# A hybrid decoder step on one core: output projection of the prompt inside the sampled tokens' stage, pages through rings

## The chip, the cores and the metric

The kernel runs on one core of a Trainium2 chip. The metric is the device time of one execution in microseconds; three runs of the kernel before gave a median of 1904.42 us (1900.69 to 1908.21). The engines are TensorE (PE, its weight loads PEld), VectorE (DVE), ScalarE (ACT), GpSimd (POOL) and SyncE (SP, which only issues transfers here). Each works through its own program in order and waits on semaphores.

## What is computed

One inference step of a two-layer decoder trunk, for 1024 prompt tokens and for 8 x 8 sampled tokens: a short gated convolution layer, then a forgetting-attention layer over a shared K and V. The sampled tokens attend to 1024 past rows in a paged pool, eight pages of 128 rows for each of eight batches, and to themselves. Width 1024, 16 heads of 64, all in float32.

```python
def forgetting_attn_layer(x, g, w_in, w_out, attend):
    h = rmsnorm(x, g)
    q, z = jnp.split(h @ w_in, 2, axis=-1)
    o = attend(q.reshape(Bg, T, N_HEADS, HEAD_DIM))
    y = o.reshape(Bg, T, D_ATT) * jax.nn.silu(z)
    return x + y @ w_out
...
x = x + jax.nn.sigmoid(x @ w_ple_gate[i]) * (p[i].astype(x.dtype) @ w_ple_proj[i])
...
k_past = cache_k[page_table].reshape(db, -1, N_HEADS, HEAD_DIM)
v_past = cache_v[page_table].reshape(db, -1, N_HEADS, HEAD_DIM)
s_past = jnp.einsum('bqhd,bkhd->bhqk', q, k_past).astype(jnp.float32) * scale
s_past = s_past + cn_q + jnp.swapaxes(rest, 1, 2)[:, :, None, :]
p = jax.nn.softmax(jnp.concatenate([s_past, s_new], axis=-1), axis=-1)
o = jnp.einsum('bhqk,bkhd->bqhd', p[..., :P].astype(v_past.dtype), v_past)
```

## The kernel before

Activations lie transposed, features on partitions and the 1088 token columns (1024 of the prompt, 64 sampled) along the free side, in eight rows of 128 features. A product in full precision is three matmuls of a faster kind: high part of the weights with the high and the low part of the activations, then low part of the weights with the high part (`w_hi`, `w_lo`, `Hhi`, `Hlo`). ScalarE makes high parts by a copy, VectorE low parts by a subtraction. A tile is 128 output features: 8 rows x 3 blocks of columns (364, 364, 360) x 3 matmuls.

The program is written by hand engine by engine, with semaphores between them. The stages around the change, in order:

- Prompt attention, eight pairs of heads (`half_pair`, twice a pair), with dense tiles of the next pair between its steps; the last pair's second half has none left. POOL normalises the blocks of P (line 537). The gated output `yT` of a pair is stored to memory (`parked_y`, line 417); the residual stream X was parked in memory earlier.
- The sampled tokens' stage, lines 881 to 1000 on TensorE. For each batch of eight: eight pages of K are turned on TensorE (`k_turn`, line 887), copied to `KT` by ScalarE (1261) and VectorE (1647), and multiplied with the queries two pages at a time (`s_scores`, 908). A bias matmul (`s_bias`, 896) starts the scores from `Bkeys` and `Arows`. VectorE finds the maximum (1682), ScalarE does exp (1272), P is turned back (924, 921) and multiplied with the pages of V (`s_values`, 939); the output is turned (945) and gated into `zsS`.
- K pages go through four buffers, loaded by SP from line 391 or 451 once a buffer is turned. V pages have two whole sets of eight, loaded by POOL (line 542): 13 of them already during the last half pair of the prompt attention, between its normalisations, then eight after each batch. `Bkeys` and the new V rows have two buffers too. Sixteen tiny loads at line 444 bring the new keys' sums to one partition row.
- After the last batch the parked rows of `yT` and X come back, Y is split into parts (1055, 1367), and eight output projection tiles over all 1088 columns follow (`out_tiles`, lines 620 to 622), then `feed`: the turning and splitting of the layer's input embedding, a split of X, and eight gate and projection tiles. The final norm and the output transposes end the program.

## Time and profile before

| | |
|---|---|
| median of three runs | 1904.42 us |
| the profiled execution, its own time | 1904.6 us |
| its span | 1902.6 us |
| TensorE busy, share of the span | 1721.6 us, 90% |
| VectorE, ScalarE, POOL busy | 867.0, 674.3, 321.1 us |
| mean granted clock of TensorE | 0.949 |
| moved by DMA | 161.87 MB, 85 GB/s on average |

The page divides the span into 40 slices; the sampled tokens' stage is slices 31 to 35, where DMA rises to nine tenths and the granted clock of TensorE falls to six. Durations of pipelined matmuls overlap in the records, so the pace of a series is read from the differences between starts, and a busy TensorE isn't necessarily at its peak. What an engine waited for stands in brackets behind a row, with the idle time before it.

### The profile page before, as it was taken

How to read it: one execution, taken by the hardware profiler on the slowest of the kernel's cores; microseconds unless marked ns; L12 is line 12 of the kernel's file. 1: busy time of each engine (PE TensorE's matmuls, PEld its weight loads, DVE VectorE, ACT ScalarE, POOL GpSimd, SP SyncE). 2: the span in 40 equal slices, each digit the busy share in tenths (PEclk: the TensorE clock that was granted, in tenths of full speed). 3: DMA queues.
4: the chain of work that ended last, by engine and by line, in shares of the span. 5: the costliest groups of instructions: out<-in, count | busy, mean ns of one | idle time of the engine just before them, and what ended most of it. 6: DMA issues, size and time to landing. Idle time of an engine off the chain costs nothing.

```text
span 1902.6 us, 31400 instructions
## 1 busy us (share of the span) xinstructions
PE 1721.6 (90%) x11034; PEld 1584.1 (83%) x11034; DVE 867.0 (46%) x1361; ACT 674.3 (35%) x1094; POOL 321.1 (17%) x335
## 2 busy tenths in 40 slices
PE   6999999999999859999999999999865888899997
PEld 5999999999989759888888888888643555598997
DVE  4433333343253484555565555555543333423443
ACT  5111111111053233555655556565531232302322
POOL 4111111100000021322222122222121222000110
PEclk8999999999999879999999999999866999899998
DMA  4111111111201203211101021110235799821102
GB/s 142 46 46 45 46 44 45 44 36 44 76 28 44 88 19 93 58 46 35 57 23 59 21 79 45 34 57 24 68 144 173 281 373 362 303 68 41 42 28 94
DMA packets 165110, 161.87 MB, mean 85 GB/s; under 512 B 19661, under 2 KB 141661, under 8 KB 164935
## 3 DMA queue, kind: packets, MB, share of 16 engines
q1 hardware_dynamic: 154566, 126.38, 21.0%
q0 software_dynamic: 10496, 34.88, 5.0%
q8 instruction: 28, 0.46, 0.1%
q14 instruction: 20, 0.16, 0.0%
HBM read 137.41 MB, written 23.81 MB: 85 GB/s over the span
## 4 chain that ended last, share of the span: by engine, by line
PE 74%; DVE 9%; issue 5%; ACT 5%; DVEq 2%; DMA 2%; ACTq 1%; SPq 1%; POOL 1%; POOLq 0%
PE PS L620 14%; PE PS L622 14%; PE PS L621 14%; PE PS L781 4%; PE PS L782 4%; PE PS L783 4%; PE PS L840 3%; PE PS L887 3%; PE PS L828 2%; PE PS L939 2%; PE PS L811 2%; DVE small L1522 2%; DVE pTl L1533 2%; PE PS L812 1%; PE PS L908 1%
## 5 line engine op out<-in xcount | busy, mean ns | idle before, releaser
L620 PE MATMUL PS<-Hhi,w_hi 128*128 128x364 f32 (+1 forms) x1536 | 513.1, 334 | 36.2 <-DVE Hlo L1367 32.9
L622 PE MATMUL PS<-Hhi,w_lo 128*128 128x364 f32 (+1 forms) x1536 | 510.7, 333 | 0.0
L621 PE MATMUL PS<-Hlo,w_hi 128*128 128x364 f32 (+1 forms) x1536 | 510.3, 332 | 0.0
L620 PEld LDWEIGHTS PS<-Hhi,w_hi 128*128 128x128 f32 x1536 | 294.9, 192 | 41.1 <-issue 29.1
L621 PEld LDWEIGHTS PS<-Hlo,w_hi 128*128 128x128 f32 x1536 | 295.0, 192 | 0.0
L622 PEld LDWEIGHTS PS<-Hhi,w_lo 128*128 128x128 f32 x1536 | 294.2, 192 | 0.0
L781 PE MATMUL PS<-Hhi,w_hi 128*128 128x364 f32 (+1 forms) x768 | 274.6, 358 | 0.1
L782 PE MATMUL PS<-Hlo,w_hi 128*128 128x364 f32 (+1 forms) x768 | 252.6, 329 | 0.0
L783 PE MATMUL PS<-Hhi,w_lo 128*128 128x364 f32 (+1 forms) x768 | 252.6, 329 | 0.0
L505 POOL TENSOR_TENSOR w_raw<-w_raw,GT 128x1024 f32<-128x1024 f32 x65 | 127.1, 1956 | 697.2 <-DMA w_raw<-in_w_kv 385.6
L1014 ACT ACTIVATE w_hi<-w_raw 128x1024 fp32r<-128x1024 f32 (+1 forms) x97 | 105.5, 1089 | 371.2 <-PE PS L622 368.5
L1317 DVE TENSOR_TENSOR w_lo<-w_raw,w_hi 128x1024 fp32r<-128x1024 f32 (+1 forms) x97 | 125.9, 1298 | 78.7 <-ACT w_hi L1014 76.4
L1533 DVE TENSOR_TENSOR pTl<-PS,pTh 128x512 fp32r<-128x512 f32 x192 | 103.6, 555 | 126.0 <-ACT pTh L1159 123.7
L537 POOL TENSOR_SCALAR Pb<-Pb,small 128x128 f32<-128x128 f32 (+7 forms) x128 | 97.3, 764 | 365.1 <-DVE small L1527 365.0
L1151 ACT ACTIVATE Pb<-PS,small 128x128 f32<-128x128 f32 (+7 forms) x128 | 94.8, 741 | 161.3 <-DVE small L1522 161.3
L781 PEld LDWEIGHTS PS<-Hhi,w_hi 128*128 128x128 f32 x768 | 147.1, 192 | 0.9 <-DVE w_lo L1317 0.4
L782 PEld LDWEIGHTS PS<-Hlo,w_hi 128*128 128x128 f32 x768 | 146.2, 190 | 0.0
L783 PEld LDWEIGHTS PS<-Hhi,w_lo 128*128 128x128 f32 x768 | 145.1, 189 | 0.0
L1159 ACT ACTIVATE pTh<-PS 128x512 fp32r<-128x512 f32 x192 | 89.9, 488 | 99.9 <-PE PS L828 96.6
L1522 DVE TENSOR_REDUCE small<-PS 128x1 f32<-128x128 f32 (+7 forms) x128 | 95.8, 749 | 39.3 <-PE PS L814 38.7
L887 PE MATMUL PS<-ident,Kpages 128*128 128x128 f32 x512 | 82.2, 309 | 34.0 <-ACT KT L1261 22.8
L887 PEld LDWEIGHTS PS<-ident,Kpages 128*128 128x128 f32 x512 | 62.4, 156 | 58.3 <-ACT KT L1261 25.9
(247 smaller groups left out, 2207.3 us busy)
## 6 DMA issues: line engine op xcount, KB each, us to landing
Kpages<-in_cache_k SPq DMA_DIRECT2D x64, 512.0 KB, 7.0
Vpages<-in_cache_v POOLq DMA_DIRECT2D x64, 512.0 KB, 9.8
w_raw<-in_w_in_a SPq DMA_DIRECT2D x64, 256.0 KB, 3.0
w_raw<-in_w_ple_gate SPq DMA_DIRECT2D x16, 512.0 KB, 3.7
w_raw<-in_w_kv SPq DMA_DIRECT2D x32, 256.0 KB, 3.2
w_raw<-in_w_in_b SPq DMA_DIRECT2D x32, 256.0 KB, 3.4
parked_x<-X SPq DMA_DIRECT2D x8, 544.0 KB, 5.2
X<-parked_x SPq DMA_DIRECT2D x8, 544.0 KB, 7.5
```

The source lines that it names most:

```text
L505: g.tensor_tensor(w, w, GT[:, :, r:r + 1].to_broadcast([P, KC, P]), ALU.mult).then_inc(sems["w_gained"], 1)
L620: mm(out, wh, hi[:, k, s:e], start=(k == 0), stop=False)
L621: mm(out, wh, lo[:, k, s:e], start=False, stop=False)
L622: last = mm(out, wl, hi[:, k, s:e], start=False, stop=(k == nk - 1))
L781: mm(out, wh, Hhi[:, k, s:e], start=(k == 0), stop=False)
L782: mm(out, wh, Hlo[:, k, s:e], start=False, stop=False)
L783: last = mm(out, wl, Hhi[:, k, s:e], start=False, stop=(k == KC - 1))
L887: last = tp(PS[:, c, (i % 4) * P:(i % 4 + 1) * P], Kr[:, pg % RING, i * P:(i + 1) * P], ident[:, :])
L1014: af(whi[:, par, 0:nk, :], raw[:, par, 0:nk, :], ACT.Copy).then_inc(sems["w_hi"], 1)
L1317: tt_(wlo[:, par, 0:nk, :], raw[:, par, 0:nk, :], f(whi[:, par, 0:nk, :]), ALU.subtract).then_inc(sems["w_split"], 1)
L1522: ve.reduce_max(small[:, qb:qb + 1], score_bank(qb)[:, 0:n], AXX, negate=True).then_inc(sems["rowmax"], 1)
L1533: tt_(pTl[:, kb % 2, q0 * P:512], PS[:, 5 + kb % 2, q0 * P:512], f(pTh[:, kb % 2, q0 * P:512]), ALU.subtract).then_inc(sems["p_lo"], 1)
```

## The change

The projection of the prompt's 1024 columns no longer has a stage of its own. Tile m runs during batch m+1 of the sampled tokens, in 16 pieces (2 blocks of 512 columns x 8 rows) of three matmuls that `out_pieces` puts between page turns, scores and values. Values of a batch are multiplied during the next batch's turns, a page or two per slot. So V needs a ring of four pages, as K has: POOL loads page n+4 when page n has been multiplied. `KT` holds single pages, scores are made page by page, page turns go to PSUM banks 5 and 6. `Bkeys`, `Arows` and the new V rows have one buffer each; the new keys' sums are stored so that one transfer per batch brings them. Everything moved into memory that the prompt attention uses, so K and V loads wait until its scores and its value products are done, and no V load stands in POOL's attention loop. The parked rows of `yT` come straight into `Hlo` and are split in place during batch 0; X comes back a row per batch. The sampled columns are projected at the end, from weights loaded unsplit into the buffers that have become free, in plain fp32 matmuls of 64 columns. The diff, cut to its core:

```diff
 RING = 4
 NK = KEYS + DS
...
-                        load_keys(0, pg, first=True)
+                    sp.wait_ge(sems["y_out"], START["y_out"] + 16 * (NPAIR - 1))
+                    for k in range(NPAIR - 1):
+                        sp.dma_start(f(Hlo[:, k, 0:SEQ]), d["y"][k]).then_inc(sems["y_back"], 16)
+                    return
                 sp.wait_ge(sems["o_done"], START["o_done"] + 4 * j + 4)
                 sp.sem_inc(sems["sp_step"], 1)
                 sp.dma_start(d["y"][bass.ds(j, 1)].rearrange("a p n -> (a p) n"), yT[:, 0:SEQ]).then_inc(sems["y_out"], 16)
...
-            sp.wait_ge(sems["y_out"], START["y_out"] + 16 * NPAIR)
-            sp.wait_ge(sems["kv_out"], START["kv_out"] + 64 * NPAIR)
...
-            with nc.allow_non_contiguous_dma(reason="eight values of each head, once"):
-                for x in range(2):
-                    for b in range(DB):
...
+            def load_x(m, par):
+                sp.dma_start(at_pair(X, m).rearrange("p a n -> p (a n)"), d["x"][bass.ds(m, 1)].rearrange("a p n -> (a p) n")).then_inc(sems[f"x_back{par}"], 16)
+            def sample_loads(b, par, x=True, tile=True, more=True):
+                if x:
+                    load_x(b, par)
+                for pg in range(RING, PAGES):
+                    load_keys(b, pg)
+                if tile:
+                    load(N_B2 + b + 1, (N_B2 + 1 + par) % 2, w_out_b[:, :, bass.ds(P * b + P, P)])
+                if more:
+                    for pg in range(RING):
+                        load_keys(b + 1, pg)
...
+            sp.wait_ge(sems["score"], START["score"] + 16 * NPAIR)
+            for pg in range(RING):
+                load_keys(0, pg, first=True)
+            sp.wait_ge(sems["pv"], START["pv"] + 24 * NPAIR)
+            load_x(0, 0)
+            sample_loads(0, 0, x=False, tile=False)
+            sample_loads(1, 1)
+            with sp.Fori(0, 2) as i:
+                sample_loads(2 * i + 2, 0)
...
+            sp.wait_ge(sems["s_score"], START["s_score"] + PAGES * DB)
+            load_last(0, KT[:, 0, :, :])
+            load_last(1, KT[:, 1, :, :])
...
+                sp.wait_ge(sems["s_pv"], START["s_pv"] + PAGES * DB - RING + u + 1)
+                load_last(3 + u, Vb[:, u, :].rearrange("p (k n) -> p k n", k=KC))
+            load_last(7, PsT[:, 0:PAGES, :])
...
-            def load_values(b, par, pg):
+            def load_values(b, pg):
...
-            def early_values(n):
-                for pg in range(n, n + 2):
-                    if pg < PAGES + 5:
...
-                    if not more and hh == 1:
-                        g.wait_ge(sems["s_table"], 16)
-                        g.wait_ge(sems["block_done"], START["block_done"] + B_B2)
                     for qb in range(4):
                         normalise(8 * hh + qb, j)
-                        if not more and hh == 1:
-                            early_values(2 * qb)
...
+            def later_values(b):
+                for pg in range(RING, PAGES):
+                    used(b, pg - RING + 1)
+                    load_values(b, pg)
+            def sample_loads(b, more=True):
+                if more:
+                    g.wait_ge(sems["s_all"], b + 1)
+                    g.sem_inc(sems["pool_step"], 1)
+                    load_sample(b + 1)
+                later_values(b - 1)
+                for pg in range(RING):
+                    used(b - 1, RING + pg + 1)
+                    load_values(b, pg)
+                    if pg == 1:
+                        load_new(b)
...
+            load_sample(0)
+            g.wait_ge(sems["pv"], START["pv"] + 24 * NPAIR)
+            for pg in range(RING):
+                load_values(0, pg)
...
+                        last = tp(PS[:, 5 + c, (i % 4) * P:(i % 4 + 1) * P], Kr[:, pg % RING, i * P:(i + 1) * P], ident[:, :])
...
+            def s_scores(b, par, pg):
...
+                        last = mm(SS[32 * g_:32 * g_ + 32, P * pg:P * pg + P], qc[:, par, g_, e, :], KT[:, pg % 2, 2 * g_ + e, :],
...
-            def s_values(b, par):
-                pe.wait_ge(sems["s_osb"], START["s_osb"] + b)
-                for pg in (0, 1, 2, 3, 4, PAGES, 5, 6, 7):
...
+            def s_values(b, pg):
...
-            def sample_batch(b, par, first=False, more=True):
-                k_turn(b, 4)
...
-                s_p_turn(b, 2)
-                s_values(b, par)
...
+            def out_pieces(m, par, q0, n):
...
+                    mm(PS[:, blk, :], wh, Hhi[:, k, s:s + 512], start=(k == 0), stop=False)
+                    mm(PS[:, blk, :], wh, Hlo[:, k, s:s + 512], start=False, stop=False)
+                    last = mm(PS[:, blk, :], wl, Hhi[:, k, s:s + 512], start=False, stop=(k == KC - 1))
+                    if k == KC - 1:
+                        last.then_inc(sems["block_done"], 1)
+                return q0 + n
...
+            def sample_batch(b, par, first=False):
+                q = 0
+                back = {3: (0, 1), 4: (2, 3), 5: (4, PAGES), 6: (5, 6), 7: (7,)}
+                for u in range(PAGES):
+                    if u >= 3 and not first:
+                        s_values(b - 1, back[u][0])
+                    if u == 2:
+                        if not first:
+                            for r in range(3):
+                                s_p_turn(b - 1, r, PAGES * b + 2)
+                        s_bias(b, par)
+                        s_scores(b, par, 0)
+                        if not first:
+                            q = out_pieces(b - 1, 1 - par, q, 1)
+                    k_turn(b, u)
+                    if not first:
+                        q = out_pieces(b - 1, 1 - par, q, 1 if u >= 2 else LAG_D[u])
+                    if u == 0 and not first:
+                        s_scores(b - 1, 1 - par, PAGES - 1)
+                        if not (isinstance(b, int) and b == 1):
+                            s_y_turn(b - 2)
+                    if u >= 2:
+                        s_scores(b, par, u - 1)
+                    if 3 <= u < 7 and not first:
+                        q = out_pieces(b - 1, 1 - par, q, 1)
+                        s_values(b - 1, back[u][1])
+            pe.wait_ge(sems["s_ones"], 1)
             sample_batch(0, 0, first=True)
+            pe.wait_ge(sems["h_ready"], 40)
+            sample_batch(1, 1)
...
-            out_tiles(N_B2, ED_B2, 32)
...
+            pe.wait_ge(sems["s_out"], START["s_out"] + DB)
+            pe.wait_ge(sems["w_last"], 16 * KC)
...
+            for t, w in enumerate(slots):
+                for k in range(KC):
+                    last = mm(PS[:, 2, NS * t:NS * t + NS], w[:, k, :], zsS[:, k, :], start=(k == 0), stop=(k == KC - 1))
+            last.then_inc(sems["s_b2s"], 1)
             feed(1, N_B3, EA_B3, ED_B3, 40)
...
-            def sample_batch(b, more=True):
-                for pg in range(4, PAGES):
-                    keep_keys(b, pg)
...
+            def sample_batch(b, par, i):
+                keep_keys(b, 0)
+                keep_keys(b, 1)
+                probabilities(b - 1)
+                keep_keys(b, 2)
+                keep_keys(b, 3)
+                w_hi((N_B2 + par) % 2, B_B2 + 2 * b - 2, loaded(N_B2 + par, 2, i))
+                for pg in range(4, PAGES):
+                    keep_keys(b, pg)
+            act.wait_ge(sems["o_done"], START["o_done"] + 4 * NPAIR)
+            y_hi(NPAIR - 1, yT[:, 0:SEQ])
+            w_hi(N_B2 % 2, B_B2 - 3, loaded(N_B2))
+            for pg in range(PAGES):
                 keep_keys(0, pg)
...
+                if pg == 0:
+                    act.wait_ge(sems["y_back"], 16 * (NPAIR - 1))
+                if pg < NPAIR - 1:
+                    y_hi(pg, f(Hlo[:, pg, 0:SEQ]))
...
+            for k in range(KC):
+                y_hi(k, X[:, k, 0:SEQ])
...
+            def sample_batch(b, par, i, more=True):
...
+                keep_keys(b, 0)
+                largest(b - 1)
+                if not (isinstance(b, int) and b == 1):
+                    outputs(b - 2)
+                keep_keys(b, 1)
+                probabilities(b - 1)
+                keep_keys(b, 2)
+                keep_keys(b, 3)
+                out_block(b - 1, 1 - par, mi, 0)
+                keep_keys(b, 4)
+                w_lo((N_B2 + par) % 2, N_B2 + b)
+                keep_keys(b, 5)
+                keep_keys(b, 6)
+                if more:
+                    prepare(b + 1, 1 - par)
+                keep_keys(b, 7)
+                attended(b - 1)
+                out_block(b - 1, 1 - par, mi, 1)
+            ve.wait_ge(sems["kv_out"], START["kv_out"] + 64 * NPAIR)
+            ve.memset(f(Bk[R_CN:R_MASK, :]), 0.0)
+            ve.memset(f(Bk[R_MASK:R_END, :]), 0.0)
...
+            ve.memset(f(Bk[R_CN:R_CN + 2, :]), 1.0)
+            ve.tensor_copy(Bk[R_MASK:R_END, KEYS:], maskb[R_MASK:R_END, R_MASK:R_END])
             ve.drain().then_inc(sems["s_ones"], 1)
...
+            prepare(0, 0)
+            y_lo(NPAIR - 1, yT[:, 0:SEQ], 33)
+            w_lo(N_B2 % 2, N_B2)
+            for pg in range(PAGES):
                 keep_keys(0, pg)
...
+                if pg < NPAIR - 1:
+                    y_lo(pg, f(Hlo[:, pg, 0:SEQ]), 34 + pg)
...
+            for k in range(KC):
+                y_lo(k, X[:, k, 0:SEQ], 41 + k)
+            ve.wait_ge(sems["s_b2s"], 1)
+            tt_(X[:, :, SEQ:], PS[:, 2, :].rearrange("p (m n) -> p m n", m=KC), X[:, :, SEQ:], ALU.add)
+            ve.drain().then_inc(sems["xs_done"], 1)
...
```

On TensorE, in a steady batch of the sampled tokens' stage, two page turns and the output's turn stood in a row before (`Kpages` is the ring of K pages, `Osb` the batch's output):

```order
L885 REGISTER_ALU [waits k_in0]
L887 MATMUL PS<-ident,Kpages 128x128 [waits s_kt0]
L887 MATMUL PS<-ident,Kpages 128x128 x3
L887 MATMUL PS<-ident,Kpages 128x128 [waits s_kt1]
L887 MATMUL PS<-ident,Kpages 128x128 x3
L885 REGISTER_ALU [waits k_in1]
L887 MATMUL PS<-ident,Kpages 128x128 [waits s_kt0]
L887 MATMUL PS<-ident,Kpages 128x128 x3
L887 MATMUL PS<-ident,Kpages 128x128 [waits s_kt1]
L887 MATMUL PS<-ident,Kpages 128x128 x3
L945 MATMUL PS<-ident,Osb 128x128 [waits s_pt1,s_osb]
L908 MATMUL PS<-KT,qc 32x256 [waits s_kt1,s_kt0]
```

After the change, the same engine in the fifth slot (page 4) of a batch:

```order
L943 MATMUL PS<-ident,Kpages 128x128 [waits s_kt0]
L943 MATMUL PS<-ident,Kpages 128x128 x3
L943 MATMUL PS<-ident,Kpages 128x128 [waits s_kt1]
L943 MATMUL PS<-ident,Kpages 128x128 x3
L1010 MATMUL PS<-Hhi,w_hi 128x512
L1011 MATMUL PS<-Hlo,w_hi 128x512
L1012 MATMUL PS<-Hhi,w_lo 128x512
L964 MATMUL PS<-KT,w_raw 32x128 [waits s_kt1,s_kt0]
L964 MATMUL PS<-KT,w_raw 32x128 x7
L1007 REGISTER_ALU
L1010 MATMUL PS<-Hhi,w_hi 128x512 [waits dve_evac]
L1011 MATMUL PS<-Hlo,w_hi 128x512
```

Now a piece of the projection (L1010 to L1012, `Hhi` and `Hlo` hold the prompt's gated output) stands behind each page turn and behind the scores, and a value product of the batch before ends the slot.

On POOL, at the start of the prompt attention's last half pair, the normalisations of `Pb` had V page loads between them:

```order
L542 ISA
L542 DMA Vpages<-in_cache_v 128x1024
L541 TENSOR_LOAD pt
L541 ISA x2
L542 ISA
L542 DMA Vpages<-in_cache_v 128x1024
L537 TENSOR_SCALAR Pb<-Pb,small 128x384 [waits rinv]
L541 TENSOR_LOAD pt
L541 ISA x2
L542 ISA
L542 DMA Vpages<-in_cache_v 128x1024
```

Now, from the last four normalisations of that half pair on:

```order
L573 TENSOR_SCALAR Pb<-Pb,small 128x640 [waits rinv]
L573 TENSOR_SCALAR Pb<-Pb,small 128x768 [waits rinv]
L573 TENSOR_SCALAR Pb<-Pb,small 128x896 [waits rinv]
L573 TENSOR_SCALAR Pb<-Pb,small 128x1024 [waits rinv]
L605 DMA Bkeys<-key_bias 16x1024 [waits s_ones,kv_out,s_restout,s_table]
L606 DMA Bkeys<-key_bias 16x8
```

The normalisations follow one another, and the first transfer behind them is that of the key bias. In the steady batch a V load was one of eight behind a single wait on the batch before; each has its own wait now:

```order
L585 ISA
L585 DMA few_rows<-out_v_sample 8x1024
L541 ISA
L541 TENSOR_LOAD pt
L541 ISA x2
L542 ISA
L542 DMA Vpages<-in_cache_v 128x1024
L541 ISA
L541 TENSOR_LOAD pt
```

and in the loop over batches now:

```order
L577 ISA [waits s_pv]
L577 TENSOR_LOAD pt
L577 ISA x2
L578 ISA
L578 DMA Vpages<-in_cache_v 128x1024
L615 REGISTER_ALU
L577 ISA [waits s_pv]
L577 TENSOR_LOAD pt
L577 ISA x2
```

What moved there is the release: from the end of a batch's value products to each single page's.

## Rows read from the trace of the kernel before

**Rows 1.** Stretches: length, busy (instructions) PE, PEld, DVE, ACT, POOL, clock, DMA share, GB/s.

```profile
1427.00:1454.00 27.00, 8.06 (x33) 6.24 (x34) 9.11 (x20) 2.39 (x4) 6.55 (x13) 0.56 0.52 169
1481.00:1645.00 164.00, 137.47 (x1538) 89.29 (x1536) 63.25 (x134) 46.52 (x81) 40.54 (x78) 0.92 0.93 346
1662.00:1749.00 87.00, 86.88 (x524) 86.20 (x524) 20.79 (x31) 7.63 (x7) 0.00 (x0) 1.00 0.20 61
```

**Rows 2.** Timeline, last half pair: start, us, what, count, idle before and releaser.

```profile
1396.82 1.76 PE L828 MATMUL PS<-ident,Pb 128*128 128x128 f32 x7 [3.90 <-POOL Pb L537]
```

**Rows 3.** Timeline, from the end of prompt attention to the first bias matmul.

```profile
1425.98 0.69 DVE L1542 TENSOR_TENSOR yT<-yT,zf 64x512 f32<-64x512 f32 x1
...
1428.04 1.78 DVE L1702 MEMSET Bkeys<- 72x2064 f32 x1 [0.38 <-issue]
...
1434.35 0.53 POOL L583 DMA_DIRECT2D Bkeys<-key_bias  x1 [21.75 <-DVEq L1713]
...
1440.18 11.65 SPq L444 DMA_DIRECT2D few_rows<-new_key_sums  x16
...
1453.80 1.23 PE L896 MATMUL PS<-Bkeys,Arows 72*128 72x512 f32 x3 [14.25 <-DVEq L1657]
```

**Rows 4.** Timeline of TensorE in a steady batch.

```profile
1522.66 1.04 PE L924 MATMUL PS<-ident,Ps 128*128 128x128 f32 x8
...
1525.44 2.37 PE L939 MATMUL PS<-Vpages,PsT 128*32 128x256 f32 x40
...
1529.73 1.09 PE L887 MATMUL PS<-ident,Kpages 128*128 128x128 f32 x8
...
1537.40 1.09 PE L887 MATMUL PS<-ident,Kpages 128*128 128x128 f32 x8
1538.42 1.07 PE L908 MATMUL PS<-KT,qc 128*32 128x256 f32 x16
1539.43 1.09 PE L887 MATMUL PS<-ident,Kpages 128*128 128x128 f32 x8
1542.91 3.32 PE L887 MATMUL PS<-ident,Kpages 128*128 128x128 f32 x13 [2.39 <-ACT KT L1261]
```

**Rows 5.** Timeline of a 512-column pair in the prompt attention, full clock.

```profile
1335.44 0.19 PEld L840 LDWEIGHTS PS<-pTh,VS 128*128 128x128 f32 x1
1335.60 0.39 PE L840 MATMUL PS<-pTh,VS 128*128 128x512 f32 x1
...
1335.83 0.39 PE L840 MATMUL PS<-pTl,VS 128*128 128x512 f32 x1
```

**Rows 6.** V pages' tile: issues (ns min/median/max), landing; then one issue.

```profile
L542 POOL DMA_DIRECT2D Vpages<-in_cache_v x64: 527/530/749, 1389.4 to 1613.8; - x64
...
DMA to landing us min/median/max: 3.7/9.8/15.0
...
1490.46 0.53 POOL L542 DMA_DIRECT2D Vpages<-in_cache_v  x1 [0.71 <-issue]
```

**Rows 7.** Single lines and tiles: ns min/median/max, first and last start, forms.

```profile
L1647 DVE COPY KT<-PS x64: 680/692/693, 1433.9 to 1632.4; 128x512 f32<-128x512 f32 x64
...
L1367 DVE TENSOR_TENSOR Hlo<-X,Hhi x16: 1282/1285/1293, 529.6 to 1761.9; 128x1088 fp32r<-128x1088 f32 x16
...
L756 PE MATMUL PS<-ones,LFP x56: 275/275/275, 700.1 to 707.6; 128*128 128x128 f32 x56
...
L756 PE MATMUL PS<-tri,LFP x16: 270/275/275, 699.9 to 707.8; 128*128 128x128 f32 x16
```

**Rows 8.** Timeline of TensorE, first gate tile of the last layer.

```profile
1755.05 0.67 PE L620 MATMUL PS<-Hhi,w_hi 128*128 128x364 f32 x1 [3.10 <-DVE Hlo L1367]
1755.51 0.51 PE L621 MATMUL PS<-Hlo,w_hi 128*128 128x364 f32 x1
1755.81 0.51 PE L622 MATMUL PS<-Hhi,w_lo 128*128 128x364 f32 x1
...
1769.87 0.33 PE L620 MATMUL PS<-PTh,w_hi 128*128 128x364 f32 x1
```

401 lines of the change are left out of this document (196 added, 205 removed).

## The prediction

> **What bounds the kernel now.** I read the profiled execution from its end backwards into stages, first by the table of stretches: busy time of each engine, granted clock, DMA share and GB/s. In [rows 1] the reader is to see that TensorE is the engine of every stretch, but in two manners. In the output projection (87 us from 1662) it is busy 86.88 of 87 us at clock 1.00 with DMA at a fifth: a pure TensorE stage. In the sampled tokens' stage (164 us from 1481) DMA is busy 0.93 of the time and moves 346 GB/s, and TensorE, though it shows as busy, has holes and clock 0.92. So one stage waits for data while the next only computes. The first 27 us of the sampled stage are the worst: TensorE busy 8.06 us at clock 0.56.
>
> Next the order of time around that start. [rows 2]: in the last half pair of the prompt attention, TensorE stood still for 3.90 us until POOL had normalised the fourth block; POOL was late because page loads of V stood between its normalisations. [rows 3]: attention ends at 1426.7 (1425.98 + 0.69). Then VectorE fills Bkeys with 1.78 us memsets, POOL may only then load the key bias, and SP issues 16 tiny transfers in 11.65 us; the first bias matmul starts at 1453.80 after 14.25 us of TensorE idle.
>
> Last, one steady batch on TensorE [rows 4], read by the differences of starts: turning a K page 1.02 us (1537.40 to 1538.42), scores of a pair of pages 1.01, turning P with the next bias and one pair of scores 2.78 (1522.66 to 1525.44), nine value products 4.29, and one hole of 2.39 us until ScalarE has done exp and then a KT copy.
>
> **The change, stage by stage.** The sum compares the stretch from the end of attention (1426.7) to the end of the first gate tile of the last layer, 1769.9 by the start of the next matmul, at 1769.87 [rows 8]: 343.2 us. Before and after that stretch the same instructions stand in the same order, but for a few small VectorE operations and a finer store near 716, that I count as nothing (TensorE has dense tiles there; if not hidden, 2 us).
>
> (a) *End of attention.* V page loads leave POOL's queue, so the 3.90 us hole goes. What is late next is TensorE itself, still in the scores of the fifth block until 1392.9 (1396.82 less the hole): minus 3.8. Bounds 0 and 5.
>
> (b) *Start and batch 0.* One buffer instead of two halves the memset of 1.78 [rows 3]; three of 0.9 in a row and drains give 3.2 us until the bias may load. Five POOL issues of 0.5 and a landing of at most 3.7 (the fastest V page, [rows 6]) make 9.7; bias and first scores, 11. The 16 tiny loads are gone. Now VectorE also makes the low parts of the prompt's output: per page a KT copy of 0.69 and 1.285 x 1024/1088 = 1.21 [rows 7], so 2.0 a page, 12 for the other six. At half clock TensorE itself would need 3 a page, 18. Taken 14: batch 0 takes 25 us (bounds 23 and 30). ScalarE's half is lighter; the seven parked rows were fetched long before.
>
> (c) *Batches 1 to 7.* Each now carries one projection tile: 16 pieces of three matmuls of 512 columns. One takes 0.23 us (1335.60 to 1335.83, [rows 5]), a piece 0.69, a tile 11.0. The batch's old work, by [rows 4]: 8 x 1.02 = 8.2; eight single-page scores of 0.5 = 4.0 (half the columns, twice the calls; a call could keep more than half its cost, at most +4); turns and bias 2.78 - 1.01 = 1.8; values 4.3; output turn 0.2. Together 18.5 to the rounding, with the tile 29.5. The old holes vanish for this reason: every KT copy (0.69) now has a piece and scores in front of the next need. Exp: the last scores end at 1539.43, the turn after the hole starts at 1542.91, 3.5 us later, of which some 0.6 are the KT copy; so P is ready 2.9 us after the scores, and a page turn with three pieces (3.1) now covers that. DMA per batch: 8.4 MB of pages, 1.1 of X row and weights, 0.1 of bias, 9.6 MB; at 346/0.93 = 372 GB/s that is 25.8 us, under TensorE's 29.5. I add 1.4 us for semaphores, exp and a marginal page: 30.9 us, times seven 216.3. Bounds 29.5 and 33 (the old hole of 2.39 stays and a little more). SP's queue has X rows, K pages and weights in line; none of their waits is for work that TensorE has not long done, since K is four pages (over 12 us) ahead. VectorE has some 13 us of work, ScalarE 10.
>
> The ring is the tight place. Page 4 of V may be issued when page 0 was multiplied; by the order that is two slots (each turn, two pieces, scores, two values = 3.84 us) less one product, 7.2 us ahead of its use. Of these POOL takes 0.53 + 0.71 = 1.24 [rows 6] and something for the signal; 6.0 are left for the landing. The fastest landing is 3.7, the median 9.8, the longest 15.0 [rows 6], but those are bursts of eight pages at a DMA share of 0.93; here three or four half-megabyte transfers meet, 3.7 + 2.5 = 6.2. So I take the fast end and a marginal wait (0.4 of the 1.4).
>
> By the Trainium skill, DMA: Bandwidth & Descriptors, Anatomy of one DMA, a load from POOL takes 2.0 us and its bytes over 436 GB/s, 3.2 us for a page. The trace's fastest is 3.7; by the page's figure the marginal wait goes and the sum is 3 us less.
>
> VectorE's low-part operation of a weight tile (1.2 us, from SBUF) now falls beside V loads. The 64 V issues of the kernel before took 527 to 749 ns [rows 6], so none was held up by a whole operation. [...]
>
> (d) *Tail.* Batch 7's tile has no page turns beside it: 11.0 + scores 0.5 + turns 1.2 + values 4.3 = 17.0. Exp is covered less (0.9), and pages 4 to 7 of V have only 2.8 us from release to use while weights and inputs of the last layer load too: 4.5 us. Sum 22.4, bounds 18 and 28.
>
> (e) *Junction.* The sampled columns get their own 64 fp32 matmuls, two passes each. The nearest row: 72 passes (56 and 16) with 128x128 weights and 128 columns, their starts from 699.9 to 707.8 [rows 7], 0.11 each, so 14.1 us; with half the columns at the least 7.1. Taken 10.6, and 1 for the last weights. Beside it ScalarE and VectorE split the prompt's X: 8 x 1.21 + 0.8 = 10.5, hidden. Then the add (0.7) and the turning of the layer's embedding (some 4, from the 6.4 us between the end of the old tiles, 1748.6, and 1755.05, less the two first splits): 16.3 in all, bounds 12.5 and 20.
>
> (f) *First gate tile.* Before, 14.8 us (1755.05 to 1769.87), since its first matmuls ran at the low clock, 0.30 apart (1755.51 to 1755.81), against 86.88/524 = 0.166 at the high one [rows 1]: 72 x 0.166 = 11.9. Its splits are done already, but the engine comes from a thin stretch again: 13.0. The same rise costs once more at batch 1: 1.5.
>
> Sum: -3.8 + 25 + 216.3 + 1.5 + 22.4 + 16.3 + 13.0 = 290.7 against 343.2: 52.5 us less. From the profiled execution, 1904.6 us with a span of 1902.6 (2.0 around it), that gives 1852.1. The median of the runs, 1904.42, is the same within 0.2. Put otherwise: some 95 us of tiles, as 88, go into the stage, whose batch grows from 164/7 = 23.4 to 31 us, and the start gets shorter.
>
> **Rivals.** *The ring of V waits at the median landing.* With 9.8, page 4 is 3.8 us late in each of seven batches, 26.6 us less the 3 counted: 1876 to 1879 with the tail. For it: the median row, and three transfers at once. Against it: the bursts are gone.
>
> *Slower.* Same place, bad price: if the landing is L, the wait is L - 6.0 a batch, and about L - 3.8 in the tail beyond what I count. Seven batches and the tail eat 52.5 at L = 13; slower by 0.5% needs L of 14. At the longest row, 15.0, it is 63 + 11 - 3: 1923. Against it: with DMA at 9.6 MB in 31 us or more, 310 GB/s, queues are shorter than at 346, and they shorten as the stage stretches.
>
> *The pieces don't pack.* Each piece stands behind a foreign matmul; if its first weight load (0.19, [rows 5]) is bare 16 times a batch, that is +3.0, and +21 in seven: 1873. For it: the pieces' own cadence is known only among their like. Against: turns and scores alternate in [rows 4] at no visible price.
>
> *The tile finds little room,* since TensorE was 0.84 busy there: the spans of pipelined matmuls overlap, and the true work is 18.5 of 23.4 us. If all the busy time were real (137.47 of 164 us, [rows 1]), a batch would be 19.6 + 11.0 + 1.4 = 32.0, not 30.9, and the total 1860; inside my range.
>
> **How the numbers follow.** Forecast, 1838 to 1864: 0.60. Less than 1838 (packing better, half-price scores, short junction): 0.07. Pieces don't pack: 0.13. Ring at about its median: 0.12. Ring between, no change: 0.04. Ring slower: 0.04. Low bound: batches at 29.5 (-10), start -2, tail -4, junction -4, clock -1: 1831. High bound: the old exp hole in seven batches (+14) or the ring at its median, with a long tail: 1882. A measurement can tell some 0.5% (10 us) from no change; faster 0.92, same 0.04, slower 0.04.
>
> **What would show it.** Right: TensorE's clock near 1.0 from batch 1 on; value-finish to value-finish 31 us; DMA share about 0.75; V pages landing in 4 to 7 us; no POOL release in front of the last half pair's turns; sampled-column matmuls 0.06 to 0.11 apart. Wrong: TensorE idle with a DMA of Vpages as releaser, once a batch, means the ring; idle by ScalarE's exp means my cover was short; scores of single pages above 0.7 us means the halved call doesn't halve. The prediction fails as a whole if batches exceed 38 us.

## The result, and the profile of the changed kernel

| | |
|---|---|
| before, median of four runs | 1906.2 us |
| changed kernel, median of four runs | 1881.9 us (1881.25 to 1885.36) |
| ratio | 0.988, 95% interval 0.9855 to 0.9906 |
| profiled execution of the changed kernel | span 1879.6 us, mean clock 0.955 |

The change makes the kernel faster, by 23 us in the profiled executions (spans of 1902.6 and 1879.6). The forecast was 52.5. The difference lies in the tail of the sampled tokens' stage and behind it, not in its batches, so the stretches of the changed kernel come first: length, busy PE, PEld, DVE, ACT, POOL, then granted clock, DMA share, GB/s.

```profile
1422.00:1448.00 26.00, 17.50 (x204) 13.11 (x204) 19.37 (x28) 13.77 (x18) 7.82 (x15) 0.80 0.74 249
1448.00:1665.00 217.00, 216.06 (x2364) 146.90 (x2362) 78.25 (x146) 53.53 (x91) 48.06 (x92) 1.00 0.84 296
1665.00:1694.00 29.00, 23.30 (x165) 12.95 (x163) 7.34 (x17) 3.23 (x5) 2.63 (x5) 0.82 1.03 302
1694.00:1733.00 39.00, 31.62 (x148) 30.69 (x149) 14.09 (x18) 11.82 (x16) 0.00 (x0) 0.61 0.17 44
1733.00:1746.00 13.00, 13.00 (x71) 13.00 (x70) 2.44 (x2) 3.26 (x5) 0.00 (x0) 0.87 0.17 52
```

The second row is the stage that the change is about: TensorE is busy 216.06 of 217 us at clock 1.00, where it had 137.47 of 164 at 0.92 [rows 1]. The fourth row is the surprise. Between the last projection tile of the prompt and the first gate tile lie 39 us in which TensorE shows as busy 31.62 us, at a clock of 0.61, with a DMA share of 0.17 and the other engines busy for a third of it.

The timeline of TensorE from the tail to the end of the first gate tile (start, us, instructions, count, idle before and releaser). A *pass* is one record of an fp32 matmul of the sampled columns; each such matmul leaves two:

```profile
1681.70 1.08 PE L992 MATMUL PS<-Vpages,PsT 128*32 128x256 f32 x8 [5.31 <-DMA Vpages<-in_cache_v]
...
1693.56 0.40 PE L1012 MATMUL PS<-Hhi,w_lo 128*128 128x512 f32 x1
1699.24 7.05 PE L1073 MATMUL PS<-zsS,KT 128*128 128x64 f32 x32 [5.28 <-DMA PsT<-in_w_out_b]
1706.08 3.62 PE L1073 MATMUL PS<-zsS,Ps 128*128 128x64 f32 x16
1709.50 13.86 PE L1073 MATMUL PS<-zsS,Vpages 128*128 128x64 f32 x64
1723.15 3.62 PE L1073 MATMUL PS<-zsS,PsT 128*128 128x64 f32 x16
1726.56 1.06 PE L782 MATMUL PS<-ident,scrA 128*128 128x128 f32 x4
...
1732.65 0.43 PE L671 MATMUL PS<-Hhi,w_hi 128*128 128x364 f32 x1 [1.88 <-DVE PTl L1566]
...
1746.24 0.33 PE L671 MATMUL PS<-PTh,w_hi 128*128 128x364 f32 x1
```

The 128 fp32 passes of the sampled columns start 27.3 us before what follows them (1699.24 to 1726.56), 0.213 each, against 10.6 in the forecast. The wait ahead of them and a stretch in their middle show the clock:

```profile
1693.50:1699.20 5.70, 0.46 (x2) 0.03 (x1) 4.08 (x4) 4.49 (x5) 0.00 (x0) 1.00 1.17 290
1703.00:1710.00 7.00, 7.00 (x35) 7.00 (x34) 1.97 (x2) 0.00 (x0) 0.00 (x0) 0.50 0.00 0
```

Half, that is 1.2 GHz, while TensorE does not stand still for a moment, and it stays so to the last pass. The records show 1.00 all through the wait and 0.50 from 1699.4 on, just after the passes have begun; 1.00 comes back at 1730, while the embedding is turned in matmuls of 128 columns. The last row of [rows 8] answers to 1746.24 here: the first gate tile ends 23.6 us earlier than before, and nothing behind it gives anything back.

### The profile page after: what moved, and what is told of

The parts are those of the page before. It is cut to its first block, busy times and chain, and to the rows that moved or that the text cites. A ratio compares the mean times of both kernels' runs of the same rounds, so it can differ in the third digit from the quotient of the medians.

```text
span 1879.6 us, 32223 instructions
## 1 busy us (share of the span) xinstructions
PE 1736.5 (92%) x11482; PEld 1573.9 (84%) x11482; DVE 859.6 (46%) x1344; ACT 672.3 (36%) x1095; POOL 324.9 (17%) x343
## 4 chain that ended last, share of the span: by engine, by line
PE 75%; DVE 8%; issue 5%; ACT 4%; DMA 3%; DVEq 2%; ACTq 1%; POOL 0%; SPq 0%; POOLq 0%
PE PS L671 13%; PE PS L673 13%; PE PS L672 13%; PE PS L835 4%; PE PS L836 4%; PE PS L837 4%; PE PS L894 3%; PE PS L943 3%; PE PS L882 2%; PE PS L865 2%; DVE small L1642 2%; PE PS L992 2%; PE PS L1010 2%; DVE pTl L1653 2%; PE PS L964 2%
## 5 line engine op out<-in xcount | busy, mean ns | idle before, releaser
L671 PE MATMUL PS<-Hhi,w_hi 128*128 128x364 f32 (+1 forms) x1344 | 447.2, 333 | 31.0 <-DVE Hlo L1476 25.8
L673 PE MATMUL PS<-Hhi,w_lo 128*128 128x364 f32 (+1 forms) x1344 | 445.6, 332 | 0.0
L672 PE MATMUL PS<-Hlo,w_hi 128*128 128x364 f32 (+1 forms) x1344 | 445.4, 331 | 0.0
L671 PEld LDWEIGHTS PS<-Hhi,w_hi 128*128 128x128 f32 x1344 | 256.8, 191 | 35.1 <-issue 23.9
L835 PE MATMUL PS<-Hhi,w_hi 128*128 128x364 f32 (+1 forms) x768 | 274.7, 358 | 0.1
L672 PEld LDWEIGHTS PS<-Hlo,w_hi 128*128 128x128 f32 x1344 | 256.7, 191 | 0.0
L673 PEld LDWEIGHTS PS<-Hhi,w_lo 128*128 128x128 f32 x1344 | 256.5, 191 | 0.0
L836 PE MATMUL PS<-Hlo,w_hi 128*128 128x364 f32 (+1 forms) x768 | 252.6, 329 | 0.0
L837 PE MATMUL PS<-Hhi,w_lo 128*128 128x364 f32 (+1 forms) x768 | 252.6, 329 | 0.0
L1108 ACT ACTIVATE w_hi<-w_raw 128x1024 fp32r<-128x1024 f32 (+1 forms) x97 | 105.5, 1088 | 311.1 <-PE PS L673 294.1
L835 PEld LDWEIGHTS PS<-Hhi,w_hi 128*128 128x128 f32 x768 | 147.1, 192 | 0.9 <-DVE w_lo L1426 0.4
L836 PEld LDWEIGHTS PS<-Hlo,w_hi 128*128 128x128 f32 x768 | 146.2, 190 | 0.0
L837 PEld LDWEIGHTS PS<-Hhi,w_lo 128*128 128x128 f32 x768 | 145.1, 189 | 0.0
L894 PE MATMUL PS<-pTh,VS 128*128 128x512 f32 x192 | 73.2, 381 | 35.2 <-DVE pTl L1653 35.1
L882 PE MATMUL PS<-ident,Pb 128*128 128x128 f32 x576 | 94.1, 284 | 6.5 <-POOL Pb L573 6.5
```

The lines of the kernel that those rows point to most:

```text
L671: mm(out, wh, hi[:, k, s:e], start=(k == 0), stop=False)
L672: mm(out, wh, lo[:, k, s:e], start=False, stop=False)
L673: last = mm(out, wl, hi[:, k, s:e], start=False, stop=(k == nk - 1))
L835: mm(out, wh, Hhi[:, k, s:e], start=(k == 0), stop=False)
L836: mm(out, wh, Hlo[:, k, s:e], start=False, stop=False)
L837: last = mm(out, wl, Hhi[:, k, s:e], start=False, stop=(k == KC - 1))
```

## The experiments

All are edits of the changed kernel, but for one. The kernel before ran beside each.

| kernel | median us | ratio to before, 95% interval |
|---|---|---|
| 1: an eighth of the passes | 1859.5 | 0.9742 to 0.9775 |
| 2: wide matmuls in the wait | 1867.0 | 0.9786 to 0.9819 |
| 3: 128 columns in a pass | 1869.8 | 0.9806 to 0.9838 |
| 4: weights first | 1875.4 | 0.9832 to 0.9865 |
| 5: embedding turned between | 1882.6 | 0.9867 to 0.9903 |
| 6: 3, 4 and 5 | 1860.4 | 0.9752 to 0.9786 |
| 7: no tile in the batches | 1856.3 | 0.9733 to 0.9787 |
| 8: 2, 4 and 5 | 1859.0 | 0.9749 to 0.9783 |
| 9: before, V loads later | 1905.5 | 0.9997 to 1.0017 |
| 10: 8, and other places in the tail | 1859.2 | 0.9744 to 0.9771 |

**1. Are the passes what the junction ends on?** They could have stood beside VectorE's splits of X and cost nothing.

```diff
             for t, w in enumerate(slots):
-                for k in range(KC):
+                for k in range(1):
...
```

The other seven eighths of that sum are left out.

> The sampled columns' own projection keeps only the first of its eight rows of features for each tile (16 fp32 passes instead of 128); the other seven eighths of that sum are left out. Everything else stands. Theory: these passes are what the junction ends on, 0.213 us each, so 112 x 0.213 = 23.9 us leave TensorE; VectorE's splits of X (until 1705) and the turning of the embedding come next, so the first gate tile starts about 20 us earlier: some 1862 us. Rival: VectorE and ScalarE end the junction anyway, the passes only stand beside them: less than 10 us, 1872 or more.

Measured 1859.5, 22.4 us less than the changed kernel: the passes are the path. 112 of them at 0.213 are 23.9 us. In the profiled execution the way from the first pass to the end of the gate tile is 21.0 us shorter (1704.16 to 1730.21, where it was 1699.24 to 1746.24): a wait in the turning grows from 0.26 to 1.66, and the gate tile takes 1.3 longer, all at the start at the low clock. The rival falls.

**2 and 3. Why is the clock low, when TensorE is busy?** Either the wait of 5.28 us ahead took the clock away, or passes of 64 columns do. The second kernel fills the wait and leaves the passes as they are; the third leaves the wait and widens the passes.

```diff
+            for i in range(26):
+                mm(PS[:, 3, :], whi[:, 0, 0, :], whi[:, 0, 0:4, :], start=True, stop=True)
             pe.wait_ge(sems["w_last"], 16 * KC)
```

> 26 extra matmuls of 512 columns, whose result nobody reads, fill the 5.3 us wait for the last weights in front of the sampled columns' passes. Theory A (the passes themselves, with 64 columns each, do not bring or keep the high clock): the wide matmuls run at 0.21 apart, and the passes behind them fall back to 0.213 apart after a few us; total within 3 us of the changed kernel's 1881.9. Theory B (the clock fell because TensorE stood still before them): the passes run 0.107 apart to the end, 128 x 0.107 = 13.7 instead of 27.3: some 1868 us.

```diff
-                    last = mm(PS[:, 2, NS * t:NS * t + NS], w[:, k, :], zsS[:, k, :], start=(k == 0), stop=(k == KC - 1))
+                    n = 2 * NS if k < KC - 1 else NS
+                    last = mm(PS[:, 6 + t // 4, P * (t % 4):P * (t % 4) + n], w[:, k, :], zsS[:, k:k + n // NS, :],
+                              start=(k == 0), stop=(k == KC - 1))
...
```

> Each fp32 pass of the sampled columns (all but those of the eighth row) moves 128 columns instead of 64; the second half is the next row's data and its result is not read. Theory A (the pace is that of the 128 x 128 weight load, and narrow passes leave the clock low): the clock rises, passes 0.107 to 0.11 apart as in the series near 700 us of the kernel before, 10 to 13 us less, 1869 to 1872 us. Theory B (the clock is low for the wait ahead): 0.213 apart as now, 1882. Theory C (columns set the pace): 0.43 apart at the low clock, +27, 1909.

The second, timeline of TensorE, then a stretch in the passes (L1075 is the pass):

```profile
1694.58 6.08 PE L1069 MATMUL PS<-w_hi 128*128 128x512 f32 x26
1700.49 3.68 PE L1075 MATMUL PS<-zsS,KT 128*128 128x64 f32 x32
1704.00 1.95 PE L1075 MATMUL PS<-zsS,Ps 128*128 128x64 f32 x16
1705.79 7.31 PE L1075 MATMUL PS<-zsS,Vpages 128*128 128x64 f32 x64
...
1714.72 0.61 PE L782 MATMUL PS<-ident,scrA 128*128 128x128 f32 x4
```

```profile
1706.00:1712.00 6.00, 6.00 (x56) 6.00 (x56) 0.00 (x0) 0.00 (x0) 0.00 (x0) 1.00 0.00 0
```

The same 128 passes take 14.2 us (1700.49 to 1714.72), 0.111 each, at clock 1.00 to the end. So theory B, measured 1867.0 against its 1868; here narrow passes don't take the clock away. The third:

```profile
1698.68 5.61 PE L1074 MATMUL PS<-zsS,KT 128*128 128x128 f32 x32 [5.04 <-DMA PsT<-in_w_out_b]
1704.13 1.95 PE L1074 MATMUL PS<-zsS,Ps 128*128 128x128 f32 x16
1705.91 7.31 PE L1074 MATMUL PS<-zsS,Vpages 128*128 128x128 f32 x64
```

```profile
1700.00:1706.00 6.00, 6.00 (x45) 6.00 (x45) 4.66 (x5) 2.09 (x3) 0.00 (x0) 0.79 0.00 0
1706.00:1712.00 6.00, 6.00 (x56) 6.00 (x55) 0.00 (x0) 0.00 (x0) 0.00 (x0) 1.00 0.00 0
```

Here the wait is there, the first 32 passes still take 5.5 us (0.17 each), and then the clock is back at 1.00 and the passes are 0.112 apart: 1869.8, as theory A said. So neither theory is the whole. Each explains one half: with the wait filled the clock stays, and behind the wait a series of 64-column passes has not brought it back in 27.3 us, though TensorE is busy without a hole, where the series of 128-column passes had it back at 1703. It takes both for the 27.3 us, and removing either gives 12 to 15 us. The third kernel also writes to other PSUM banks (6 and 7 for 2); that part of its edit wasn't tried apart. Nor do columns alone settle it: in experiment 4 the turns of 128 columns behind the passes leave the clock at 0.50, in the changed kernel it rises during the same turns. Theory C falls as well: 64 or 128 columns, a pass takes 0.11 at the high clock. What the two widths share is the weight load of 128 x 128 in fp32, so that is the likeliest limit of a pass; it wasn't tried apart.

The Trainium skill, TensorE: Matmul & The Clock Gate, Loop structure matters more than you think, says that matmuls behind long waits for transfers run at the low clock; the case agrees: 0.50 behind the wait of 5.28 us, and with that wait filled 13.1 us less for the passes (27.3 to 14.2). The same page, What's actually happening, says that the low clock is the default and that activity of TensorE releases it. If activity means that the profile shows the engine as busy, the trace does not agree: 27.3 us of it released nothing.

**4. What is late in the tail?** SyncE had issued the last layer's inputs and two gate tiles in front of most of the weights, and VectorE waited 15.01 us for the high part of the first gate tile, which ScalarE could only make once it had landed.

```diff
             load_last(0, KT[:, 0, :, :])
             load_last(1, KT[:, 1, :, :])
-            for dst, src in ((sA[:, 0:D], p_p[1][:, 0:4, :]), (sZ[:, 0:D], p_p[1][:, 4:8, :])):
...
             load_last(7, PsT[:, 0:PAGES, :])
+            for dst, src in ((sA[:, 0:D], p_p[1][:, 0:4, :]), (sZ[:, 0:D], p_p[1][:, 4:8, :])):
...
```

> SyncE issues the eight unsplit weight tiles of the sampled columns ahead of the last layer's inputs and its first two gate and projection tiles, and ScalarE and VectorE split the first gate tile after X and not before. Theory (what is late in the tail are bytes that nobody needs yet): the V wait of 5.3 us in the tail shrinks to 1 or less and the wait for the last weights of 5.3 us to 2 or less, 7 to 9 us less, 1873 to 1875 us. Rival: the ring's releases set both waits, since page 4 of V and the last four weight tiles wait for value products: 0 to 3 us less.

```profile
1678.15 0.64 PE L992 MATMUL PS<-Vpages,PsT 128*32 128x256 f32 x8 [1.85 <-DMA Vpages<-in_cache_v]
...
1693.14 7.06 PE L1073 MATMUL PS<-zsS,KT 128*128 128x64 f32 x32 [2.92 <-DMA PsT<-in_w_out_b]
```

The stretch of its passes:

```profile
1693.00:1720.50 27.50, 27.36 (x129) 27.39 (x130) 9.65 (x9) 6.88 (x7) 0.00 (x0) 0.50 0.33 89
```

Measured 1875.4, 6.5 us less: a little under the range given. Both waits shrink, by 3.5 and 2.4 us, and neither goes. For the first the cause shows: page 4 of V is issued at the same time in both (1674.49 and 1674.39), but its product starts 7.2 us later in the changed kernel and 3.8 us later here, near the fastest landing of the stage, 3.5. What is left of that wait, 1.85, belongs to the ring's release, as the rival has it. What is left of the second isn't settled: its last tiles wait for releases, but the DMA share is 1.07 from 1678 to 1693, so the rate can hold them too. And the passes behind the shorter wait, 2.92 us, run at 0.50 all the same, 0.213 apart.

**5. The turning of the embedding** moved between the passes:

```diff
-            for t, w in enumerate(slots):
+            for x, t in enumerate((3, 4, 5, 6, 0, 1, 2, 7)):
+                w = slots[t]
+                if x in (4, 6):
+                    feed_turn(1, x // 2 - 2)
...
-            feed(1, N_B3, EA_B3, ED_B3, 40)
+            feed(1, N_B3, EA_B3, ED_B3, 40, turn=False)
...
```

> The turning of the last layer's embedding moves from behind the sampled columns' passes to between them (after four of their eight tiles and after six), and VectorE makes its low parts before it waits for the passes. Theory: the first gate tile then starts as soon as the passes and their addition end, so the 6.1 us between them (1726.6 to 1732.65) shrink to 1 to 2: 4 to 5 us less, 1877. The turns are full-width matmuls of 128 columns, which could also bring the clock up in between; if they do, the passes behind them (64 of 128) run at 0.11 instead of 0.21 and 6 us more go: 1871. Rival: the first gate tile waits for the splits of its own sampled columns all the same: no gain, 1882.

```profile
1700.90 13.89 PE L1080 MATMUL PS<-zsS,Vpages 128*128 128x64 f32 x64 [5.91 <-DMA PsT<-in_w_out_b]
1714.58 1.06 PE L781 MATMUL PS<-ident,scrA 128*128 128x128 f32 x4
...
1716.72 7.09 PE L1080 MATMUL PS<-zsS,KT 128*128 128x64 f32 x32
...
1732.59 0.65 PE L671 MATMUL PS<-Hhi,w_hi 128*128 128x364 f32 x1
...
1735.12 0.64 PE L671 MATMUL PS<-Hhi,w_hi 128*128 128x360 f32 x1 [0.37 <-DVE Hlo L1583]
```

1882.6, no gain, where 4 to 5 us were expected. The edit does what it says: from the first pass to the gate tile 31.7 us, where it was 33.4. But TensorE's own part of the turning, two times 2.1 us at the low clock, doesn't vanish when it is moved, only the waits in it do. And the 1.7 us are used up on both sides: the last weights land later, so that the passes start at 1700.90 and not at 1699.24, and the gate tile takes 14.6 us (it ends at 1747.23) and not 13.6, since it still starts at the low clock and now waits 0.37 us for the low part of its own sampled columns. So the rival is right in a small part. Nor do 2.1 us of 128-column turns between narrow passes bring the clock up here: the passes stay 0.213 apart.

**6 and 8. Together**: the third, or the second with 18 wide matmuls, with the fourth and the fifth.

> 128 columns in each fp32 pass, weights of the sampled columns loaded first, and the embedding turned between the passes, together. The single runs gave 12.1 us (128 columns) and 6.5 us (weights first) against 1881.9; with 4 us for the turning, and none of them eating another's gain: 1859. If the clock rise is the same few microseconds at half pace whatever comes ahead, nothing is lost; if the turning is hidden less now that the passes are short (14 us instead of 27), 1862.

> As the version with all three (weights first, embedding turned between the passes), but with 64 columns a pass and 18 unread matmuls of 512 columns in the wait ahead of them. Wide matmuls in the wait gave 14.9 us alone and weights first 6.5; with 4 for the turning: 1857. If wide matmuls in the wait and 128 columns a pass do the same thing (hold the high clock or bring it back), this is 2 to 3 us ahead of the other version, the time that the clock needs to come back.

The second of these, timeline of TensorE:

```profile
1689.57 4.26 PE L1073 MATMUL PS<-w_hi 128*128 128x512 f32 x18
1693.67 7.25 PE L1082 MATMUL PS<-zsS,Vpages 128*128 128x64 f32 x64
...
1710.33 0.41 PE L671 MATMUL PS<-Hhi,w_hi 128*128 128x364 f32 x1
```

1860.4 and 1859.0, near the 1859 and 1857 expected. The gains of the single edits add (6.5 with 12.1 and with 14.9 give 1863.3 and 1860.5), the turning brings at most 3 us more (in both, the gate tile waits 1.24 us for the low part of its sampled columns), and the two ways to the clock cannot be told apart by their intervals. Both versions are faster than the changed kernel, by 21 to 23 us, and than the one before by 2.3%.

**7. What does the projection tile cost in a batch?**

```diff
-                    mm(PS[:, blk, :], wh, Hhi[:, k, s:s + 512], start=(k == 0), stop=False)
-                    mm(PS[:, blk, :], wh, Hlo[:, k, s:s + 512], start=False, stop=False)
-                    last = mm(PS[:, blk, :], wl, Hhi[:, k, s:s + 512], start=False, stop=(k == KC - 1))
+                    if k < KC - 1:
+                        continue
+                    last = mm(PS[:, blk, :], wl, Hhi[:, k, s:s + 512], start=True, stop=True)
```

> The prompt's output projection is left out of the batches but for the last of each block's 24 matmuls (the output of those columns is wrong in that part); 46 matmuls of 0.23 us, 10.6 us, go from each of seven batches and from the tail. Theory (TensorE sets the batch, as in the forecast): 31.3 falls to 20.7 and then meets the transfers, 9.6 MB at the 372 GB/s of the old stage, 25.8 us: so 5.5 us a batch and about 10 in the tail, 1881.9 - 38 - 8 = 1836. Rival (nothing but TensorE sets it): 7 x 10.6 + 10 = 84 less, 1798. Rival (the ring's landings set it already): under 2 us a batch, 1860 or more.

Once a batch VectorE scales its output (L1807). In the changed kernel two of these starts, five batches apart:

```profile
1508.79 0.34 DVE L1807 TENSOR_SCALAR Osb<-PS,small 128x128 f32<-128x128 f32 x1
...
1665.21 0.34 DVE L1807 TENSOR_SCALAR Osb<-PS,small 128x128 f32<-128x128 f32 x1
```

Without the tile, six batches apart; then the waits of TensorE from 1480 to 1640 (total, times, longest), and the stretch:

```profile
1475.85 0.34 DVE L1807 TENSOR_SCALAR Osb<-PS,small 128x128 f32<-128x128 f32 x1
...
1638.58 0.34 DVE L1807 TENSOR_SCALAR Osb<-PS,small 128x128 f32<-128x128 f32 x1
```

```profile
PE PS L992 <- DMA Vpages<-in_cache_v: 23.9, 6, 4.9
PE PS L975 <- ACTq L1368: 10.9, 6, 1.8
```

```profile
1481.00:1640.00 159.00, 125.53 (x1753) 85.38 (x1751) 64.07 (x122) 44.06 (x74) 41.27 (x79) 0.92 0.94 341
```

A batch takes 31.3 us with the tile and 27.1 without, so 10.6 us of matmuls cost 4.2. The rest lies over waits that exist without it: 4.0 us a batch for page 4 of V and 1.8 for exp. Measured in all is 25.6 less, not the 46 of the theory and not the 84 of the first rival.

In the batches the theory had a limit at about the right place, but what it is isn't shown. The DMA share is 0.94, as before, at 341 GB/s and not 372; that would make 27.1 us the time of 9.2 MB. But TensorE waits only for page 4 of V, never for a page of K, and that is the ring's tight place: in one batch the product of page 0 starts at 1542.16, POOL issues the loads of the next bias first and page 4 at 1545.06, and page 4's product starts at 1551.91. So page 4 is issued 2.3 us after the product of page 0 ends (1542.71), for POOL's order, and takes up to 6.9 us to land, where the fastest page of the stage took 3.7; the wait is 4.4. The rate lengthens the landing and the ring makes the wait; which of them sets 27.1 can't be told from this. The kernel before had 346 GB/s and 23.4 us, 8.1 MB. If the rate is the limit, some 3.2 of the 7.9 us by which a batch grew are the bytes that came along with the projection (an estimate, 1.1 MB of X and weights at 341 GB/s), and 4.2 are its matmuls.

In the tail the theory expected 8 to 10 us, and there the matmuls cost nothing: from the scaling of batch 6's output to that of batch 7's it is 24.4 us with the tile (1665.21 to 1689.60) and 24.3 without (1638.58 to 1662.9). The work that is left out turns into waits, 5.67 us for page 4 of V, as 5.31 with the tile, and 4.57 us for VectorE ahead of the last turn, which had itself stood 16.37 us behind the high part of the first gate tile. So what sets the tail's length here are loads, and not TensorE's work.

The same kernel shows what a piece costs between foreign matmuls. First the changed kernel, then the one without the tile, at the high clock (L943 a page turn, L964 scores, L992 value products):

```profile
1553.00 1.09 PE L943 MATMUL PS<-ident,Kpages 128*128 128x128 f32 x8
...
1554.72 0.65 PE L964 MATMUL PS<-KT,w_raw 128*32 128x128 f32 x16
...
1556.20 1.07 PE L992 MATMUL PS<-Vpages,PsT 128*32 128x256 f32 x16
```

```profile
1540.68 1.09 PE L943 MATMUL PS<-ident,Kpages 128*128 128x128 f32 x8
1541.70 0.64 PE L964 MATMUL PS<-KT,w_raw 128*32 128x128 f32 x16
1542.16 0.61 PE L992 MATMUL PS<-Vpages,PsT 128*32 128x256 f32 x8
```

From a turn to the scores it is 1.72 us with a piece between and 1.02 without, so the piece costs its 0.70. From the scores to a value product it is 1.48 and 0.46: there it costs 1.02.

**9. One part alone, in the kernel before**: the V loads taken out of POOL's normalisations.

```diff
-                        if not more and hh == 1:
-                            early_values(2 * qb)
...
+            for n in range(0, 2 * PAGES, 2):
+                early_values(n)
             for pg in range(5, PAGES):
```

> The kernel before, with one part of the change alone: no V page is loaded between POOL's normalisations; all sixteen pages of the first two batches are issued behind the key bias of batches 0 and 1. Theory (step a of the forecast): the hole of 3.9 us in the last half pair goes, TensorE is late next, attention ends some 4 us earlier. But 6.8 MB that were moved beside the attention now come at the start of the sampled stage, which moves 346 GB/s as it is: 19.7 us of transfers, of which the 27 us start can take at most half (DMA share 0.52). So the kernel gets slower by 0 to 10 us, 1904 to 1914. Rival: the start hides all of it, 4 us faster, 1900.

```profile
1427.00:1454.00 27.00, 6.56 (x43) 4.99 (x47) 5.39 (x15) 1.19 (x2) 13.60 (x26) 0.56 0.84 301
```

1905.5, ratio 1.0007: no change. The hole of [rows 2] goes and attention ends 4.6 us earlier (its last VectorE operation starts at 1421.34, for 1425.98 in [rows 3]), so step (a) is right as a mechanism. But the first bias matmul starts at 1452.23, only 1.6 us earlier than in [rows 3]: the transfers have moved into the start, whose DMA share rises from 0.52 [rows 1] to 0.84. So this part alone brings nothing. In the whole change the earlier end counts: its first bias matmul starts at 1432.33, 10.1 us after the end of attention, where it was 27.1. That it has no tiny loads and fewer bytes ahead of the first batch is the likely reason; these weren't tried apart.

**10. The last two waits of the tail.** Two weight tiles go to places that are free earlier, three trailing pieces in front of page 4's product.

```diff
+            load_last(7, Kr[:, 2, :].rearrange("p (k n) -> p k n", k=KC))
+            sp.wait_ge(sems["w_split"], START["w_split"] + N_B3)
+            load_last(3, raw[:, 0, 0:KC, :])
...
-                q = out_pieces(m, 1, q, 1)
+                q = out_pieces(m, 1, q, 4 if vs[0] == 4 else 1)
...
```

> The version with wide matmuls in the wait, weights first and the embedding turned between the passes (1859.0), and two more edits in the tail: two of the last eight weight tiles go to places that are free earlier (a K page's buffer and the raw weight buffer), so that none waits for the last value product, and three of the last tile's trailing pieces stand in front of the value product that waited 2.24 us for page 4 of V. Theory: that wait goes (2.2 us) and the last weights land 1 to 2 us earlier: 1855 to 1857. Rival: what is issued earlier competes with the last V pages (3.5 MB at some 290 GB/s in the tail) and only moves the wait: 1859 again.

```profile
1680.99 1.08 PE L1000 MATMUL PS<-Vpages,PsT 128*32 128x256 f32 x8 [2.48 <-DMA Vpages<-in_cache_v]
```

1859.2, as without the two edits: the rival. The wait had been 2.24 us; with 2.1 us more work ahead of it it is 2.48. Page 4 is issued at the same time (1674.54, and 1674.75 in experiment 8), but its product starts 6.5 us after that and not 4.1, and from issue to product the DMA engines move 327 GB/s and not 268. So what is issued earlier stands in the page's way, and the page lands later by about as much as the product could have come earlier.

## Why the forecast was wrong in size

The forecast put the end of the first gate tile at 1717.4 (1426.7 + 290.7); it came at 1746.24, 28.8 us later. The median, 1881.9, is also just what its high bound of 1882 says, but by chance: that bound was made of an exp hole in every batch or of a ring at its median landing, and neither came. By its own steps:

| step | forecast us | measured us |
|---|---|---|
| (a) end of attention | -3.8 | -4.5 |
| (b) start and batch 0 | 25 | 25.7 |
| (c) batches 1 to 7, clock rise | 217.8 | 218.7 |
| (d) tail | 22.4 | 27.2 |
| (e) junction | 16.3 | 38.9 |
| (f) first gate tile | 13.0 | 13.6 |

Measured are 1426.67 to 1422.21, then the stretches that end at 1447.9, 1666.6, 1693.8, 1732.65 and 1746.24.

**(a), (b), (c) and (f) hold**, within 1 us each. In (a) the hole of 3.90 us is gone; another POOL wait of 3.22 us in the same half pair stands in both kernels, so the sign "no POOL release" is met only for the first. In (c) two misses cancel. The batch is 31.3 and not 30.9, 2.7 us more in seven; the clock rise of 1.5 did not come, since the clock was at 1.00 from 1440 on. And the 1.4 us a batch that were taken for semaphores, exp and a marginal page went elsewhere: TensorE hardly waits (216.06 of 217 us busy), but four pieces a batch stand between scores and a value product and cost 1.02 and not 0.69 (experiment 7), 1.3 us together. The DMA share is 0.84 over the stage, and not the 0.75 that was named as a sign; its own 25.8 of 30.9 us would have been 0.83. The V ring is where it was feared and at about the price taken: pages land in 3.5, 6.7 and 8.9 us at the least, the median and the most (6.0 are free), and TensorE waited 0.9 us for them from 1480 to 1640.

```profile
DMA to landing us min/median/max: 3.5/6.7/8.9
```

The rival of the ring at its median of 9.8 falls: here the median is 6.7. That of pieces that don't pack holds for four or five of sixteen, at some 1.4 us a batch and not its 3.0. The one that the tile finds little room took 32.0 us a batch, 0.7 too long where the forecast's 30.9 was 0.4 short, but neither had the reason: the room is in waits for page 4 of V and for exp, as experiment 7 shows.

**(d) is 4.8 short.** The tail's V wait was seen, and counted with the rest at 4.5; it is 5.31 alone, and the low clock that follows it adds more (0.60 and 0.42 between the starts of a piece, at 1683.72, 1684.32 and 1684.74, where 0.23 is the pace). From 1681.7 to 1689 the clock is 0.50, and half of these 7.3 us, some 3.6, is its price by estimate; the forecast had none for it here either. Experiment 4 names the cause of the wait: 3.5 of the 5.31 us are queueing behind loads that TensorE doesn't need for over 40 us (issued until 1682.7, first used at 1726.56).

**(e) is the step that failed, by 22.6 us of 28.8.** "Taken 10.6" was a pass at 0.083, between 0.11 and half of that; measured are 27.3, at 0.213. Three things were wrong. First, the halving: the nearest row [rows 7] had 128 columns and 0.11, and the forecast let half the columns take off up to half the time. Experiments 2 and 3 show 0.11 for both widths, so that the right value was the upper bound, 14.1 (14.2 measured); this alone is 3.6 us. Second and larger, the clock: the row it leaned on was taken at the high clock (1.00 from 700 to 708 in the kernel before), and the forecast carried it to a place behind the tail and its waits without asking what clock would be granted there. It did ask that in (f) and for batch 1, and not in (e). That is another 13.1 us. Third, the wait for the last weights, taken as 1, was 5.28: another 4.3. It costs its own time, and experiment 2, which fills it, shows that the clock goes with it. 1.4 us more is the addition and the turning, 6.1 for 4.7.

With the clock held and the loads in order, the stretch from the last piece to the gate tile is 20.8 us (1689.57 to 1710.33, experiment 8), near the forecast's 16.3 and the 3.6 us of the halving. So 21 to 23 of the 29 us that the change failed to bring can be had by small edits around the junction.

## What to carry to other kernels

A price read from a row is a price at that row's clock: before a series is costed, ask what TensorE does just ahead of it, and whether such a series was ever seen to bring the clock back. A short series behind a wait can cost double, as here, and a few unread wide matmuls in the wait, or wider passes, may be the cheapest repair. A busy share doesn't show this; read the granted clock beside it. When work is moved away from a stage, what remains of it at the old place (here 64 of 1088 columns) deserves as much working as what is moved; and in a tail, put transfers in the order in which they are waited for.
